# Key norm and output variance of a delta mixer: sum and spread in one same-head product

## The reference

```python
kk = (k * k_k).reshape(B, S, H, N)
kk = kk / jnp.maximum(jnp.linalg.norm(kk, axis=-1, keepdims=True), 1e-12)
...
y = ...                                   # scan over the tokens, per head
mean = jnp.mean(y, axis=-1, keepdims=True)
var = jnp.mean(jnp.square(y - mean), axis=-1, keepdims=True)
yn = ((y - mean) * lax.rsqrt(var + RWKV_GN_EPS)).reshape(B, S, D)
yn = yn * gn_g + gn_b
...
out = (yn + bonus) * g @ w_o
```

## Time and profile before

| | us |
|---|---|
| median of 3 runs | 2159.41 (2158.1 to 2162.83) |
| profiled execution, its own time | 2161.63 |
| its span | 2159.8 |
| TensorE busy / VectorE / ScalarE / GpSimd | 2100.1 / 1521.0 / 1169.6 / 378.0 |
| mean granted TensorE clock | 0.995 of full speed |

### The profile page before, as it was taken

One profiled execution on the slowest core, in us unless ns is written; L12 is line 12 of the kernel. 1 busy time (PEld: TensorE's weight loads), 2 busy tenths in 40 slices (PEclk: granted clock), 3 DMA queues, 4 the chain that ended last, 5 costly groups with the idle time before them and its releaser, 6 DMA issues.

```text
span 2159.8 us, 40536 instructions
## 1 busy us (share of the span) xinstructions
PE 2100.1 (97%) x16664; PEld 1886.6 (87%) x16664; DVE 1521.0 (70%) x2114; ACT 1169.6 (54%) x2030; POOL 378.0 (18%) x357
## 2 busy tenths in 40 slices
PE   8999999999999999999999999999999988999998
PEld 5888988998888889889888998988888877898887
DVE  6897757788779977577776687477558544647754
ACT  4564556665546545566655575465436632446542
POOL 0141022111102110221111002120132540123001
PEclk9999999999999999999999999999999999999999
DMA  8987762467758867625566544355543400434552
GB/s 311 365 298 273 267 243 99 165 233 261 260 208 312 300 254 266 254 91 179 204 224 211 189 170 150 138 178 187 184 163 139 166 4 4 147 127 163 193 186 98
DMA packets 116679, 424.66 MB, mean 197 GB/s; under 512 B 12944, under 2 KB 14736, under 8 KB 115600
## 3 DMA queue, kind: packets, MB, share of 16 engines
q1 hardware_dynamic: 112896, 409.52, 52.6%
q10 hardware_dynamic: 3600, 12.55, 1.6%
HBM read 418.35 MB, written 3.67 MB: 195 GB/s over the span
## 4 chain that ended last, share of the span: by engine, by line
PE 83%; DVE 6%; issue 4%; ACT 4%; POOL 1%; DMA 1%; SPq 0%; POOLq 0%; ACTq 0%; DVEq 0%
PE banks L601 82%; DVE weight_lower L1736 1%; POOL heap L3030 1%; DMA weight_ring<-w_ada_dram 1%; ACT xn_t L2637 1%; ACT weight_upper L2459 1%; PE banks L1556 0%; ACT heap L2637 0%; PE banks L1135 0%; DMA weight_ring<-w_in_dram 0%; DVE nmax L1883 0%; DVE heap L2076 0%; ACT heap L2651 0%; DVE weight_ring L1747 0%; DVE heap L2142 0%
## 5 line engine op out<-in xcount | busy, mean ns | idle before, releaser
L1736 DVE TENSOR_TENSOR weight_lower<-weight_ring,weight_upper 128x1024 fp32r<-128x1024 f32 x580 | 741.9, 1287 | 262.2 <-ACT weight_upper L2459 260.5
L601 PE MATMUL banks<-xn_halves,weight_upper 128*128 128x512 f32 (+1 forms) x3680 | 806.2, 342 | 0.8 <-DVE xn_halves L2059 0.7
L2459 ACT ACTIVATE weight_upper<-weight_ring 128x1024 fp32r<-128x1024 f32 x580 | 610.1, 1058 | 291.0 <-PE banks L601 197.6
L601 PEld LDWEIGHTS banks<-xn_halves,weight_upper 128*128 128x128 f32 x3680 | 612.2, 188 | 63.9 <-issue 1.1
L601 PE MATMUL banks<-xn_halves,weight_lower 128*128 128x256 f32 x2832 | 519.3, 281 | 2.2 <-DVE weight_lower L1736 1.5
L601 PEld LDWEIGHTS banks<-xn_halves,weight_lower 128*128 128x128 f32 x2832 | 433.8, 189 | 27.5 <-DVE weight_lower L1736 2.2
L601 PE MATMUL banks<-hidden,weight_upper 128*128 128x512 f32 x1216 | 309.7, 393 | 0.6 <-DVE heap L2201 0.6
L3030 POOL TENSOR_TENSOR heap<-heap 128x256 f32<-128x256 f32 x120 | 122.2, 1023 | 872.0 <-ACT heap L2754 585.4
L601 PEld LDWEIGHTS banks<-hidden,weight_upper 128*128 128x128 f32 x1216 | 215.6, 188 | 38.0 <-DVE heap L2201 0.7
L1747 DVE CUSTOM_DVE_ANT_0 weight_ring<-weight_ring,c_rows,vecs 128x1024 f32<-128x1024 f32 x140 | 185.4, 1328 | 20.5 <-DMA weight_ring<-w_ada_dram 20.1
L601 PEld LDWEIGHTS banks<-hidden,weight_lower 128*128 128x128 f32 x1216 | 167.6, 188 | 15.2
(11 more groups left out here) (311 smaller groups left out, 2410.0 us busy)
## 6 DMA issues: line engine op xcount, KB each, us to landing
weight_ring<-w_ada_dram SPq DMA_DIRECT2D x140, 512.0 KB, 4.3
weight_ring<-ffn_gate_dram SPq DMA_DIRECT2D x88, 512.0 KB, 3.8
weight_ring<-ffn_up_dram SPq DMA_DIRECT2D x88, 512.0 KB, 4.4
weight_ring<-ffn_down_dram SPq DMA_DIRECT2D x88, 512.0 KB, 3.3
weight_ring<-m_w_up_dram SPq DMA_DIRECT2D x64, 512.0 KB, 3.2
weight_ring<-m_w_down_dram SPq DMA_DIRECT2D x64, 512.0 KB, 3.2
weight_ring<-w_in_dram SPq DMA_DIRECT2D x58, 512.0 KB, 3.4
weight_ring<-b_w_rkv_dram SPq DMA_DIRECT2D x24, 512.0 KB, 3.4
```

The source lines that it names most:

```text
L601: return nc.tensor.matmul(o, w, r, start=first, stop=last)
L1736: V.tensor_tensor(w_lo[:, n % RING, :], ring[:, n % RING, :], w_hi[:, j % SPLITS, :].bitcast(F32), ALU.subtract).then_inc(*did("weight_low ...
L2459: A.activation(w_hi[:, j % SPLITS, :], ring[:, n % RING, :], ACT.Copy).then_inc(*did("weight_upper", j))
```

## The change

`head_sum`, `widen` and `head_spread` go. Both stages use `same_head`: eight products 128x256 sum the squares and spread the sum over the features of the head. ACT takes the root of each bank, 128x512, from PSUM into `head_dev` (slot 5 of the heap). DVE inverts it there, element by element, in four steps, and multiplies; each product comes one step behind its reciprocal. The clamp at 1e-12 becomes a `min` with 1e12 in the product, and 1/64 and the epsilon become scale and bias of the root.

```diff
-                for k in range(KD - FIRST, KD):
-                    head_sum("kk", kk_sq, "kk_sq", k)
...
                 for f, (name, n, done, readers_of) in enumerate(items(0)):
                     project(name, n, xs_hl[0], done, readers_of)
                     if f in (1, 3):
                         lora_pair(2 * f - 2)
...
-                    if f == 5:
-                        head_spread("kk", at=4)
+                    if f == 0:
+                        pe.wait_ge(*of("delta_consts_in", 0))
+                        same_head("kk", kk_sq, "kk_sq", at=4, read="head_root")
...
                 same_head("mean", xn, "y_all")
                 mem_key(i, 0, 4, 0, 4)
-                for k in range(KD):
-                    head_sum("var", slot[3], "yc_sq", k)
-                    if k % 2:
-                        mem_key(i, 0, 4, 4 + k // 2, 5 + k // 2)
-                mem_key(i, 1, 5, 0, 6)
-                head_spread("var")
-                mem_key(i, 1, 5, 6, KD)
-                mem_keys(i, range(2, KD - 2))
+                same_head("var", slot[3], "yc_sq", read="head_root")
+                mem_key(i, 0, 4, 4, KD)
+                mem_keys(i, range(1, KD - 2))
```

On VectorE (kk; var is alike, with `tensor_tensor` for the product):

```diff
-                dve.wait_ge(*due("head_root", "kk"))
-                step(V.tensor_scalar(stat[:, 0, :], stat[:, 0, :], 1e-12, None, ALU.max))
-                step(V.reciprocal(stat[:, 0, :], stat[:, 0, :]))
-                widen("kk", 0)
...
-                    V.tensor_tensor(kk_t[:, ks, :], kk_t[:, ks, :], ps, ALU.mult).then_inc(
-                        *did("head_used", ("kk", b)))
+                for b in range(5):
+                    if b < 4:
+                        dve.wait_ge(*due("head_root", ("kk", b)))
+                        ks = slice(2 * b, 2 * b + 2)
+                        V.reciprocal(head_dev[:, ks, :], head_dev[:, ks, :]).then_inc(*did("head_norm", ("kk", b)))
+                    if b:
+                        dve.wait_ge(*due("head_norm", ("kk", b - 1)))
+                        dve.wait_ge(*due("kk", 2 * b - 1))
+                        ks = slice(2 * b - 2, 2 * b)
+                        V.scalar_tensor_tensor(kk_t[:, ks, :], head_dev[:, ks, :], 1e12, kk_t[:, ks, :], ALU.min,
+                                               ALU.mult).then_inc(*did("head_used", ("kk", b - 1)))
```

On ScalarE the roots of kk stand after the last `shifted_upper`, those of var after the squares:

```diff
+                def head_root(name, b, at, **more):
+                    act.wait_ge(*due("head_spread", (name, b)))
+                    A.activation(head_dev[:, 2 * b:2 * b + 2, :], bank[:, at, :].rearrange("p (k t) -> p k t", k=2),
+                                 ACT.Sqrt, **more).then_inc(*did("head_root", (name, b)))
...
+                for b in range(4):
+                    head_root("kk", b, 4 + b)
...
+                for b in range(4):
+                    head_root("var", b, b, scale=1.0 / RN, bias=const("gn_eps"))
                 keys(i, [0])
```

More of the change, by code:

```diff
@@ L74, in constant_columns @@
     c["eps"] = np.full((P, 1), EPS)
+    c["gn_eps"] = np.full((P, 1), GN_EPS)
     half = ROPE // 2
@@ L416, in program @@
         xs_hl = {0: xs_hl[0], 1: xs_hl[1], 2: xs_hl[1]}
-        wide = {n: slots(5, QT * RH * RN) for n in ("kk", "var")}
+        head_dev = slot[5]
         rkr_t, exp_plus = xn, slot[10]
@@ L1345, in mlp, with same_head @@
                 down("m_w_down", i * KF2, hid2_hl, KF2, "hidden2_lower", (i, 2), (i, 5), "mixed")
[L1347 to L1359, removed]
+            def same_head(name, src, ready, at=0, read="head_used"):
                 for k in range(KD):
@@ L1368, in same_head @@
                         mn.then_inc(*did("head_spread", (name, k // 2)))
[L1369 to L1375, removed]
-                for k in range(KD):
[L1377 to L1383, removed]
-                    if k % 2:
-                        mn.then_inc(*did("head_spread", (name, k // 2)))
-                        readers[b] = [("head_used", (name, k // 2))]
+                        readers[b] = [(read, (name, k // 2))]
             def delta_mixer(i):
@@ L2303, in delta_mixer @@
                         *did("head_used", ("mean", b)))
[L2304 to L2313 removed]
+                for b in range(5):
+                    if b < 4:
+                        dve.wait_ge(*due("head_root", ("var", b)))
+                        ks = slice(2 * b, 2 * b + 2)
+                        V.reciprocal(head_dev[:, ks, :], head_dev[:, ks, :]).then_inc(*did("head_norm", ("var", b)))
+                    if b:
+                        dve.wait_ge(*due("head_norm", ("var", b - 1)))
+                        ks = slice(2 * b - 2, 2 * b)
+                        V.tensor_tensor(xn[:, ks, :], xn[:, ks, :], head_dev[:, ks, :], ALU.mult).then_inc(
+                            *did("head_used", ("var", b - 1)))
                 for k in range(KD):
@@ L2889, in delta_mixer @@
                     xs_upper(0, f)
-                act.wait_ge(*due("head_sums", "kk"))
-                A.activation(stat[:, 0, :], bank[:, 6, 0:QT * RH], ACT.Sqrt).then_inc(
-                    *did("head_root", "kk", also=[("head_sums_read", "kk")]))
                 for k in range(KD):
@@ L2927, in delta_mixer @@
                                  ).then_inc(*did("yc_sqs", b, also=[("yc_sq", 2 * b), ("yc_sq", 2 * b + 1)]))
+                for b in range(4):
+                    head_root("var", b, b, scale=1.0 / RN, bias=const("gn_eps"))
                 keys(i, [0])
-                act.wait_ge(*due("head_var", 0))
-                A.activation(stat[:, 3, :], stat[:, 3, :], ACT.Sqrt).then_inc(*did("head_root", "var"))
                 for k in range(KD):
```

24 lines of the change are left out of this document (1 added, 23 removed).

## The result

The changed kernel takes **2179.39 us** (median of 5 runs, 2178.6 to 2180.57) against 2159.41 before: ratio **1.0087**, 95% interval 1.0075 to 1.0098, 20.0 us slower. The forecast was 2180. Timed again on another occasion, beside the experiments, it came out at 1.0095 (1.0078 to 1.0112). The profiled execution has a span of 2178.0 us.

What follows compares the result with a forecast made beforehand. TensorE bounds the kernel, 83% of the last-ending chain. Key norm +9.5, variance +4.7 and clock +6.4 sum to 20.6 us: 2182.2 by the profiled execution, 2180 us as median, range 2170 to 2190 (0.87).

Steps and rivals of the forecast that it cites:

- r0 earlier: Key norm: with the head sums removed, r0, the first projection of r, starts only 1.0 us earlier.
- idle time before the first LoRA pair: Key norm: the pair needs banks 4 to 7, so TensorE idles 4.5 us until ACT has rooted all four.
- idle time before r7: Key norm: r7, last projection of r, waits 8.1 us for its weight_lower, queued behind DVE's 15.7 us block.
- r0 to v3, clock included: Key norm, first r projection to fourth v projection: v3 shifts with r7, +9.5 us before any fall of the clock.
- mean product to b_w_o, clock included: Output variance up to b_w_o: +4.7 us for the late fifth memory key, +2.4 us for a clock fall.
- The reciprocal's price: Both stages: a RECIPROCAL of 128x512 on DVE costs 3.33 us, at 6.2 ns a column from three smaller shapes.
- The table load: ACT's roots: 1.28 us per load taken; by the skill page's 2.66 us each stage would lose 1.4 us more.
- The clock: TensorE's clock falls in three idle stretches, costing 1.6, 2.4 and 2.4 us, +6.4; bounds 0 and about 3.3 each.
- The fifth key: Output variance: the fifth memory key waits for ACT's copy of key 1; TensorE idles 10 us, b_w_o comes 4.7 later.
- The plain-rate rival: Both stages: wide reciprocals stream like other DVE steps, 0.68 us each; 2155.3 to 2156.9 us; chance 0.08.
- the dearer reciprocals: Rival: wide reciprocals cost a third more than the line, GpSimd working beside DVE, 8.8 us more: 2189 us; chance 0.08.
- PEclk of the page: Sign: the profile page's TensorE clock value would be below 9 in the slices near 1700 and 1860.

Runs made afterwards that it cites:

- dummy products: Changed kernel plus never-read 128x128 products, 18 before the first LoRA pair, 34 before r7, 38 before the fifth key; ratio 1.0057 to before.
- run without the inversion: Changed kernel with each of the eight 128x512 RECIPROCALs replaced by a constant multiplication of the same shape, result not the reference's; ratio 1.0011 to before.

## Why the prediction was right

Step by step, with what was measured in the kernel after:

| step | forecast | measured |
|---|---|---|
| RECIPROCAL 128x512, by the line through the earlier trace rows | 3.33 us | 3.33 us |
| product 128x256, 16 passes | 3.3 us | 3.45 us |
| VectorE's block of four reciprocals and four products | 15.7 us | 15.4 us (kk), 15.3 us (var) |
| four roots on ACT | 2.1 us | 2.07 us |
| r0 earlier | 1.0 us | 0.9 us (r0 starts 7.03 us earlier than in the first trace of before, VectorE's steps near 1640, ahead of the change, 6.17) |
| idle time before the first LoRA pair | 4.5 us, released by ACT's root | 4.23 us, ACT L2832 |
| idle time before r7 | 8.1 us, weight_lower | 8.15 us, weight_lower |
| r0 to v3, clock included | 63.8 us (49.33 + 9.5 + 1.0 + 4.0) | 64.81, 64.93 us |
| idle time before the fifth key | 10 us, ACT's key copy | 9.07 us, ACT L2701 |
| mean product to b_w_o, clock included | 39.9 us (32.80 + 7.1) | 39.16, 38.84 us |
| clock, kk and var | 4.0 and 2.4 us | 4.4 and 2.3 us |

**The reciprocal's price** carried the whole forecast, and three small shapes in the trace gave it within 1%. From 32 to 512 columns the measured slope is 6.2 ns a column, as between the small ones. The prediction's reading of the Trainium skill (VectorE: DVE Perf Modes, "First, the fixed hardware budget") with its "repeat count of 8" as eight cycles a column was an estimate of 4.4 us, and the measurement decides against it. At 4.4 us four reciprocals would have made r7 wait 4 us longer.

**The table load** cost 1.28 us in each place, as the rows of before had it. The Trainium skill (ScalarE: Activation LUTs, "What ACT_TABLE_LOAD costs") gives the same 1283 ns for the load and adds 1380 ns of drain, 2.66 us in all; from the start of a load to the next ACTIVATE these traces have 1.30 us at most where nothing else is waited for, so the drain isn't seen in them.

**The clock** was the least secure term (bounds 0 and 10) and came out well, which the dummy products show and the first trace alone could not. Its sum was right in the kk stretch and its division was not: 1.6 us were taken for the fall before the first pair and 2.4 for that before r7. Against the run with dummy products the first trace of after has 2.8 us from the first pair to the second (14.04 and 11.23) and 1.6 from r7 to v3 (14.63 and 13.01); the second trace has 1.7 (12.88) and 2.4 (15.42).

**The sum** is nearer than its terms. The kk stretch cost 14.6 us in the first traces (64.81 less 49.33, less the 0.9 of r0) where 13.5 was forecast, the variance 6.4 where 7.1 was; the two errors are of opposite sign.

What was off:
- **The fifth key.** The prediction put the 4.7 us down to ACT's copy and spoke of no further wait. Measured without the clock it is 4.1 (36.86 less 32.80), but the reason given was only the first of two: with that wait gone, 7.5 us of it come again at `b_w_o`, from the same block of VectorE. The idle time itself was 9.07 us and not 10: the head sums of the variance, counted as 4.0 us, took 3.25 by the starts of their rows before, so TensorE reached the fifth key's wait later. Where the key starts hangs on ACT's copy, so the +4.7 didn't suffer by it.
- **The plain-rate rival** was priced 5 us too low. It forecast 2155.3 to 2156.9, 2.5 to 4.1 us below before; the run without the inversion came out 2.4 above. 3.5 us of that are the kk stretch, of which 2.1 are GpSimd and VectorE getting in each other's way, which the prediction had looked at only under the dearer reciprocals, and 1.1 the clock. Against the 2156.9, which has the fall of the clock in it, 1.4 us are left; the interval of the run (0 to 4.7) is wider than that. Had a reciprocal been as cheap as a product, the change would still have won nothing.
- **Places that the change doesn't touch.** Before the marks the profiled execution of after is 6.2 us ahead of that of before, 5.0 of it by 400 us (before has falls of the clock near 290 and near 390, after one near 260) and all of it by 880 us; in the delta core it is 3.2 us slower. So 3.2 of the 6.2 cancel: the two profiled executions differ by 18.2 us, the medians by 20.0. The forecast was worked from one execution, and such differences are larger than its error of 0.6 us on the 20; that it came so near is in part luck.
- **PEclk of the page.** It was to drop below 9 in slices near 1700 and 1860. The page has 9 in all 40: a slice is 54 us long, and 7 to 10 us at half speed in it leave its mean at 0.90 or more. Falls of this size are seen in the short stretches only.

## What to carry to other kernels

A statistic that is inverted after it is spread costs by its columns: 32 columns were 0.35 us, 512 are 3.33, and what the merged product saved on TensorE (some 3.5 us in the key norm, inside its waits) did not pay for it. Look for who stands in the queue behind such a block: here the loss was not the products of the block itself but a `weight_lower` and a bank that had to wait for it. If the elementwise form is wanted, put it on an engine that is idle at that place (the Exp of half the negative Ln on ACT cost the variance nothing and won 4 us; in the key norm, where ACT is busy, the version with the same eight steps was 3 to 5 us longer than before at the better of two places), and ask after each wait removed which one stands behind it.

## What was not expected of the hardware

- A long RECIPROCAL on VectorE left GpSimd's steps at 0.73 us, while a dense run of multiplications and weight_lowers stretched one of them to 4.22.
- Falls of the clock come and go between executions of the same kernel: in the delta core 0 and then 3.3 us for before, near 850 and 1220 us in some traces and not in others. A single trace settles a difference of 3 us only if the stretches at half speed are counted first.
- Filling idle time with 90 products that nobody reads made the changed kernel 6 to 8 us faster.
